# The next four experts' tokens gathered behind the third expert's up product, and their gate matrix turned behind the first's

## What is computed

```
def run_block(args):
    xb, e = args
    return (jax.nn.silu(xb @ w_gate[e]) * (xb @ w_up[e])) @ w_down[e]

out = jnp.zeros((n, d), jnp.float32).at[row_token].add(ys.astype(jnp.float32) * row_gate[:, None])
```

## Time and profile before

| | |
|---|---|
| three runs | 1033.83, 1035.26 and 1036.64 us; median 1035.26 |
| profiled execution | 1035.04 us, of which the span of the core 1033.3 us |
| expert stage | from 255 us (first gather) to 718 us |
| TensorE busy | 795.7 us, 77% |
| VectorE, ScalarE, GpSimd busy | 443.0, 325.7 and 75.5 us |
| queue of the weight loads | 285.38 MB, 70.3% of 16 engines' span |

### The profile page before, as it was taken

The page is one execution under the profiler, slowest core; times in us unless marked ns, Lnnn a source line. Parts: engine busy times, 40 slices in busy tenths (PEclk is TensorE's granted clock), DMA queues, the critical chain, the costliest instruction groups (busy, mean ns, idle before and its releaser), DMA issues.

```text
span 1033.3 us, 16106 instructions
## 1 busy us (share of the span) xinstructions
PE 795.7 (77%) x6814; PEld 629.3 (61%) x6814; DVE 443.0 (43%) x754; ACT 325.7 (32%) x520; POOL 75.5 (7%) x100
## 2 busy tenths in 40 slices
PE   5999999985667466546557547576898979999996
PEld 4978998765424243322424214243887779999995
DVE  4855848554313031311213112134747655455554
ACT  4754345631010001001001000102485454444443
POOL 1008433100000000000000000000001000000000
PEclk9999999995969678886889778788999989999999
DMA  5895244356799999999899999999843544565101
GB/s 206 260 386 178 95 154 162 131 213 274 317 427 428 427 410 392 427 427 426 351 427 426 429 426 375 426 428 356 316 133 113 183 162 163 175 209 188 41 1 41
DMA packets 69735, 287.05 MB, mean 278 GB/s; under 512 B 11505, under 2 KB 34334, under 8 KB 57374
## 3 DMA queue, kind: packets, MB, share of 16 engines
q1 hardware_dynamic: 69346, 285.38, 70.3%
q10 hardware_dynamic: 316, 0.58, 0.2%
HBM read 284.90 MB, written 1.05 MB: 277 GB/s over the span
## 4 chain that ended last, share of the span: by engine, by line
PE 48%; issue 28%; DMA 14%; DVE 5%; ACT 3%; POOL 1%; ACTq 0%; POOLq 0%; SPq 0%; DVEq 0%
PE bank L557 13%; DMA down_a<-in_w_down_dram 13%; PE bank L1926 7%; PE bank L1913 7%; PE bank L591 5%; PE bank L1898 4%; PE bank L1939 4%; PE bank L569 3%; DMA ring<-in_w_in_dram 1%; DVE w_lo L542 1%; PE bank L1744 1%; ACT w_hi L532 1%; DVE h_m L1521 1%; PE bank L1757 1%; PE bank L1873 1%
## 5 line engine op out<-in xcount | busy, mean ns | idle before, releaser
L557 PE MATMUL bank<-act_p,w_hi 128*128 128x256 f32 x1440 | 268.3, 288 | 9.8 <-issue 5.8
L542 DVE TENSOR_TENSOR w_lo<-ring,w_hi 128x1024 fp32r<-128x1024 f32 x138 | 178.9, 1297 | 157.2 <-ACT w_hi L532 157.0
L557 PEld LDWEIGHTS bank<-act_p,w_hi 128*128 128x128 f32 x1440 | 227.9, 194 | 14.0 <-issue 9.2
L532 ACT ACTIVATE w_hi<-ring 128x1024 fp32r<-128x1024 f32 x138 | 145.9, 1058 | 195.8 <-PE bank L557 136.2
L557 PE MATMUL bank<-act_p,w_lo 128*128 128x256 f32 x720 | 205.5, 285 | 0.0
L557 PEld LDWEIGHTS bank<-act_p,w_lo 128*128 128x128 f32 x720 | 139.9, 194 | 0.0
L1529 DVE COPY y_e<-bank 32x256 f32<-32x256 f32 x64 | 27.2, 425 | 194.4 <-PE bank L1926 194.0
L1926 PE MATMUL bank<-down_b,h_t 128*32 128x256 f32 x512 | 48.4, 544 | 79.7 <-issue 74.0
L591 PE MATMUL bank<-w_hi,act_q 128*128 128x512 f32 x304 | 95.3, 394 | 0.4 <-issue 0.4
L1048 ACT ACTIVATE y_e<-bank 32x256 f32<-32x256 f32 x64 | 23.9, 373 | 218.3 <-PE bank L1926 217.9
L1913 PE MATMUL bank<-ring,x_t 128*32 128x256 f32 x1536 | 89.4, 385 | 0.0
(11 more groups left out here) (330 smaller groups left out, 879.9 us busy)
## 6 DMA issues: line engine op xcount, KB each, us to landing
ring<-in_w_up_dram SPq DMA_DIRECT2D x24, 2048.0 KB, 21.7
ring<-in_w_gate_dram SPq DMA_DIRECT2D x24, 2048.0 KB, 17.3
ring<-in_w_in_dram SPq DMA_DIRECT2D x16, 2048.0 KB, 18.7
down_b<-in_w_down_dram SPq DMA_DIRECT2D x16, 2048.0 KB, 25.5
down_a<-in_w_down_dram SPq DMA_DIRECT2D x16, 2048.0 KB, 24.2
ring<-in_w_ffn_in_dram SPq DMA_DIRECT2D x22, 1024.0 KB, 6.6
pair_d<-in_w_gate_dram SPq DMA_DIRECT2D x8, 2048.0 KB, 26.8
pair_d<-in_w_up_dram SPq DMA_DIRECT2D x8, 2048.0 KB, 31.3
```

Source lines behind the costliest of these rows:

```text
L532: nc.scalar.activation(parts(w_hi, g, view), view, ACT.Copy).then_inc(split_hi, 1)
L542: nc.vector.tensor_tensor(parts(w_lo, g, view), view, h, ALU.subtract).then_inc(split_lo, 1)
L557: mm = nc.tensor.matmul(dst, parts(wt, g, grans[g][1])[:, k, :], a[:, x_part, k, :], start=(k == 0 and i == 0), stop=(k == KC - 1 and i == 2))
```

## The change

Three things move. The gather is taken out of the group's start: group 0's stands once ahead of the loop, and that of group `k` + 1 behind the up product of group `k`'s third expert (`e == 2`), ahead of its down product. It runs in every group, so the last group gathers for a group that does not follow; its masks are built in any case, and nobody reads the result. VectorE keeps the gathered tokens at the same place, behind the third expert's `h_t`. The two transposes of the gate matrix go behind the first expert's up product, and write bank 4 in place of bank 5; VectorE keeps `gmat` behind the first expert's `h_t`. VectorE's building of the next masks goes behind the first expert's output copies. The number of instructions in the loop stays the same, and the loads of SyncE and their waits are untouched.

```diff
+        def gather(k, s):
+
+            pe.wait_ge(built, 4 * k + 2)
+            for half in range(2):
+                for c in range(4):
+                    for b in range(TB):
+                        o = (4 * half + c) * P
+                        mm = nc.tensor.matmul(bank[5 + half][:, c * P:(c + 1) * P], tok[:, b, o:o + P],
+                                              onehot[:, s, b, :], start=(b == 0), stop=(b == TB - 1))
+                mm.then_inc(xt_raw, 1)
+
+        gather(0, 0)
         with pe.Fori(0, n_rounds) as r:
...
-                    pe.wait_ge(built, 4 * k + 2)
-                    for half in range(2):
-                        for c in range(4):
-                            for b in range(TB):
-                                ...
-                        mm.then_inc(xt_raw, 1)
                     pe.wait_ge(xt_kept, 2 * k + 2)
-                    pe.wait_ge(built, 4 * k + 4)
-                    for b in range(TB):
-                        mm = nc.tensor.transpose(bank[5][:, b * P:(b + 1) * P], gated[:, b, :], ident[:, :])
-                    mm.then_inc(gmat_raw, 1)
                     for e in range(4):
...
                         mm.then_inc(gu_raw, 1)
+                        if e == 0:
+                            pe.wait_ge(built, 4 * k + 4)
+                            for b in range(TB):
+                                mm = nc.tensor.transpose(bank[4][:, b * P:(b + 1) * P], gated[:, b, :], ident[:, :])
+                            mm.then_inc(gmat_raw, 1)
+                        if e == 2:
+                            gather(k + 1, 1 - s)
                         pe.wait_ge(ht_kept, x + 1)
```

On VectorE the same in its list:

```diff
+        def keep_xt(k, s):
+            for half in range(2):
+                dve.wait_ge(xt_raw, 2 * k + half + 1)
+                nc.vector.tensor_tensor(
+                    x_t[:, s, 4 * half:4 * half + 4, :],
+                    bank[5 + half][:, :].rearrange("p (c j) -> p c j", c=4),
+                    bcast(g_ffn[:, 4 * half:4 * half + 4].unsqueeze(2), [P, 4, P]), ALU.mult).then_inc(xt_kept, 1)
+
         build_group(0, 0)
         nc.vector.memset(sm[:, 67:68], 0.0).then_inc(moe_added, 1)
+        keep_xt(0, 0)
...
-                    for half in range(2):
-                        dve.wait_ge(xt_raw, 2 * k + half + 1)
-                        ...
-                    dve.wait_ge(gmat_raw, k + 1)
-                    nc.vector.tensor_copy(gmat[:, :], bank[5][:, 0:T]).then_inc(gmat_kept, 1)
-                    dve.wait_ge(built, 4 * k + 4)
-                    build_group(1 - s, k + 1)
...
                         nc.vector.transpose(h_t[:, :], h_m[:, :]).then_inc(ht_kept, 1)
+                        if e == 0:
+                            dve.wait_ge(gmat_raw, k + 1)
+                            nc.vector.tensor_copy(gmat[:, :], bank[4][:, 0:T]).then_inc(gmat_kept, 1)
+                        if e == 2:
+                            keep_xt(k + 1, 1 - s)
                         dve.wait_ge(ye_raw, x + 1)
...
                         ins.then_inc(ye_dve, 1)
+                        if e == 0:
+                            dve.wait_ge(built, 4 * k + 4)
+                            build_group(1 - s, k + 1)
```

## The result

| | before | after |
|---|---|---|
| median of 4 runs | 1035.26 us | 1024.12 us (1022.82 to 1025.21) |
| profiled execution, span | 1033.3 us | 1022.6 us |
| ratio of the runs, 95% interval | | 0.9885 (0.987 to 0.990) |

The change makes the kernel faster by 1.15%, 11.1 us between the medians and 11.9 by the ratio; 8.3 were forecast. The forecast was 1026.8 us and its range began at 1023.5: the median lies 0.6 us inside, the time by the ratio, 1023.4, just outside. Run again on another chip beside the experiments (e5) it took 1023.79 us, 0.9872 (0.9856 to 0.9888).

A forecast was written before the change was run, and what follows sets the result against it. The prediction took the expert stage as bound by the DMA stream, run dry by TensorE after loop returns. Its terms, -0.4 - 10.3 + 2.4 = -8.3 us from 1035.04, gave a forecast of 1026.8 us, range 1023.5 to 1031.0.

The forecast's parts named there:

- What bounds the kernel: Expert stage: the DMA stream sets the time; TensorE counts only where it makes the stream run dry, after loop returns.
- (1): First group: the two gate transposes leave the path to the first product, which the stream awaits: -0.4 us.
- (2): Loop returns: with the gather gone from ahead of the first product, loads issue 4.1 us earlier, recovering dry time: -10.3 us.
- The dry time: Expert stage: four 10 us windows, all following loop returns, lack 10.9 us of stream against 427 GB/s.
- (3): Gather ahead of the third expert's down product, seven times: hidden in the wait for that matrix, 1.7 us spare, no cost.
- (4): Last group: the gather for a group that does not exist is exposed ahead of the third down product: +2.4 us.
- (5): End of the stage: the last group's second down matrix lands earlier by what the stream recovers, and TensorE is in time.
- (6): VectorE: building the next masks, 2.69 us, is hidden in a 2.90 us idle; the other moved pieces cost nothing.
- The rule of the Trainium skill: Code cached in 16 KB lines of 256 instructions: loop start moves to the next line, loads 9 us earlier, sum 0.5 better.
- Rival C: Expert stage: too few expert buffers dry the stream, so the 10.9 us stay: +2.0 us, 1037.0 us; chance 0.05.
- A: Only part comes through: exposed gather at half clock, or loop entry costs an idle piece: 1030.3 or 1031.3 us; chance 0.14.
- B: Loop returns: a third idle piece of about 5.5 us falls into the first product: +5.9 us, 1040.9 us; chance 0.07.

The follow-up runs named there:

- e2: The changed kernel with 192 more TensorE instructions (small unread matmuls) ahead of the loop, putting the loop at its old place in a code piece: 1026.83 us, 0.9909.
- e4: The changed kernel with the gather and the keeping of its tokens behind the second expert's up product instead of the third's: 1022.42 us, 0.986.
- e1: The kernel before, order untouched, with 32 more TensorE instructions (8 small unread matmuls) ahead of the loop: 1022.17 us, 0.9857.
- e8: The kernel before with 128 more TensorE instructions (32 small unread matmuls) ahead of the loop: 1024.85 us, 0.9895.
- e3: The changed kernel with 64 more TensorE instructions (16 small unread matmuls) ahead of the loop: 1027.31 us, 0.9914.
- e6: The kernel before with only 8 more TensorE instructions (2 small unread matmuls) ahead of the loop: 1036.16 us, 0.999.

## Why the prediction was wrong

The sign, the place and the mechanism by which TensorE dries the stream were right. The size was some 3 us short, and what removed the dryness was not what the forecast counted on: it kept the idle pieces and moved work out from behind them, and the idle pieces themselves went.

- *What bounds the kernel.* Right: with the stream at 428 GB/s throughout, the stage falls into step with it, and the end of the kernel follows. Everything behind 682 moved as a block.
- *(1), -0.4.* Right within 0.2: from the first gather to the first loads it was 11.45 us (255.25 to 266.70), now 10.91 (255.69 to 266.60). Of the 0.54, 0.28 is the gather itself (6.34 and 6.06), which leaves 0.26. The wait for the kept tokens, with the loop's entry in it, is 0.99 us against 0.87; no idle piece of code stands there.
- *(2), -10.3: the step that failed.* It held "If the second idle piece falls where it does now", and never asked whether the pieces would come at all. They were taken as a property of the return; they were one of the loop's size and address. Measured from the first group's fourth down product to the last group's second (300.18 to 695.00, now 299.93 to 682.17), the stage is shorter by 12.6 us, for -10.3. With the idle pieces kept, in e2, it is 386.2 us (298.56 to 684.80) against 394.8 before: 8.6 shorter. So under its own condition the term was too large, since each fetching round still costs 1.5 us, and the condition did not hold, which gave 4.0 us more.
- The dry time itself was sized at 10.9 us from four windows at 427 GB/s. Over the whole stretch, 416 against 428 GB/s, it is 12/428 x 410 = 11.5 us. The windows beside the four (418 at 490, 413 at 390) held the rest. The 27 pieces of code are 0.44 MB, by estimate another 1.0 us at that rate.
- *(3), the gather in its cover: nothing.* Right: in the first group 1.76 us of the wait were left.
- *(4), +2.4.* Measured 1.9 between the traces before and after, and 2.3 against e4. The difference is the product ahead of the gather, 4.87 us before and 4.38 after; in e4 it is 4.44.
- *(5) and (6).* Right. TensorE waited 9.35 us for the last group's second down matrix. The releaser there reads "issue" too, but it is the matrix: it was issued at 656.49, and these loads take 25.6 us to land, which is 682.1. The prediction's sentence that idle pieces with this releaser stand at the returns and nowhere else is too strong; those that no load explains do.
- *The rule of the Trainium skill.* The prediction counted with the piece of 256 instructions and left it at the point where it would have decided; it still kept the first idle piece (loads some 9 us earlier, 16.9 measured). The Trainium skill, Advanced Engine Details and Errata, section ISA Cache, gives TensorE 128 KB for code. With lines of 16 KB that makes eight, an estimate from the page's figures. The loop is 852 records of matmuls and weight loads a group, so 2 x 852 = 1704 instructions, 6.7 lines, and somewhat more with waits. Begun 16 instructions ahead of a line's end, as before, it touches eight lines by this count; begun 16 (e1) or 48 (the changed kernel) behind a line's start, seven. By the page's figure alone both would fit. The runs say that only seven do: 9 pieces at each of 3 returns are the 27 by which 61 exceeds 34, and at seven lines none. Nine for a loop of eight lines would be explained by one line that is fetched ahead. The changed kernel's first round agrees, with seven pieces from 259.3 to 348.9 us, though the first of its seven lines was already there (the gather that runs into it at 255.69 has no idle piece). No run shows the fetching ahead by itself.
- *Rival C* had the right question and the wrong answer: the dry places did have another cause than the order, but not the buffers.
- *Rivals A and B.* Neither came. B's reason against it was sound: e2 has no third idle piece.
- *Two slips in the sums.* 1035.04 - 8.3 + 0.2 is 1027.0, not 1026.8, and 695.0 less the 10.7 us of (1) and (2) is 684.3, not 684.5. Neither matters.

## What to carry to other kernels

Here, idle pieces with the releaser "issue" at a loop's return, together with a code queue that brought pieces again at each round, meant that the loop did not fit where its code is kept; such a trace is worth a look there before work is moved. Moving instructions across the loop's start can then change the time for a reason that has nothing to do with what it computes, so such a change is to be compared with the old order at the new address. In this kernel eight useless matmuls did what the reordering did, and the order's own price (a gather for nobody) could then be taken back.

## What the runs showed of the hardware that I had not expected

- The loop was fetched whole or not at all: 9 pieces of 16.4 KB in a round, or none, and a shift of its start by 32 instructions (e1) decided it.
- Under a full DMA stream a piece of code takes about 5 us to come: 371.87 to 377.35 before, 370.44 to 375.69 in e2. The transfer is the smaller part: in the first idle piece of the kernel before (367.2 to 371.87) the packet starts at 369.1 and takes 1.07 us.
- A round that fetches costs the full stream 1.5 us, with no window visibly short (e8, e3).
- The same loop can fetch at some returns and not at others: one of three in e8, two of three in e3, all three in the kernel before, e2 and e6.
